# The second feed-forward's up projection as seven half-size products in eight of eleven steps, with its row factor in the operand and some arithmetic on GpSimd

## The reference

```python
h = rms_norm_2(x, norm_ffn_g[l])
up = causal_dwconv(h @ w_up[l], conv_ffn_w[l])      # w_up: 1024 x 5632, three taps along the tokens
a, b = jnp.split(up, 2, axis=-1)                    # 2816 channels each
x = x + (jax.nn.silu(a) * b) @ w_down[l]
```

## Time and profile before

| | |
|---|---|
| median of 3 runs | 1296.87 us (1295.75 to 1297.6) |
| the profiled execution's own time | 1296.4 us |
| its span in the profile | 1294.7 us |
| granted TensorE clock over the span | 0.999 of full speed |
| busy: PE, DVE, ACT, POOL | 98%, 69%, 45%, 10% |
| first up projection, PE | 240.2 to 461.0 us |
| second up projection, PE | 932.7 to 1175.7 us |

### The profile page before, as it was taken

One profiled execution on the slowest core, in us unless ns is written; L12 is line 12 of the kernel. 1 busy time (PEld: TensorE's weight loads), 2 busy tenths in 40 slices (PEclk: granted clock), 3 DMA queues, 4 the chain that ended last, 5 costly groups with the idle time before them and its releaser, 6 DMA issues.

```text
span 1294.7 us, 17058 instructions
## 1 busy us (share of the span) xinstructions
PE 1270.2 (98%) x6810; PEld 1064.7 (82%) x6810; DVE 893.9 (69%) x1062; ACT 588.5 (45%) x704; POOL 130.6 (10%) x120
## 2 busy tenths in 40 slices
PE   7999999999999999999999999999999999999997
PEld 5777677789999899998888888668888888888876
DVE  6788655887888688887536433658665656668796
ACT  6372672564554445564311322563433333336555
POOL 4003010013222010200000002000300000001020
PEclk9999999999999999999999999999999999999999
DMA  5422101259999497823433332102222222256765
GB/s 168 136 75 88 66 1 59 88 147 179 202 197 179 106 236 230 151 63 113 163 98 98 98 98 98 65 1 74 91 97 97 97 97 97 97 186 104 205 107 137
DMA packets 120708, 151.81 MB, mean 117 GB/s; under 512 B 4170, under 2 KB 93498, under 8 KB 120514
## 3 DMA queue, kind: packets, MB, share of 16 engines
q1 hardware_dynamic: 91906, 108.92, 25.2%
q0 software_dynamic: 28720, 41.96, 19.1%
q10 hardware_dynamic: 16, 0.00, 0.0%
HBM read 148.76 MB, written 2.11 MB: 117 GB/s over the span
## 4 chain that ended last, share of the span: by engine, by line
PE 95%; DVE 2%; ACT 2%; DMA 0%; issue 0%; SPq 0%; ACTq 0%
PE psum L1897 20%; PE psum L1899 20%; PE psum L1898 20%; PE psum L2158 4%; PE psum L2159 4%; PE psum L2160 4%; PE psum L2202 3%; PE psum L2354 3%; PE psum L2204 3%; PE psum L2356 3%; PE psum L2355 3%; PE psum L2203 3%; PE psum L2037 1%; PE psum L2022 1%; PE psum L2268 1%; PE psum L2049 1%
## 5 line engine op out<-in xcount | busy, mean ns | idle before, releaser
L1897 PE MATMUL psum<-act_hi,w_hi 128*128 128x512 f32 x968 | 385.1, 398 | 4.2 <-DVE act_lo L1191 1.7
L1898 PE MATMUL psum<-act_lo,w_hi 128*128 128x512 f32 x968 | 378.6, 391 | 0.0
L1899 PE MATMUL psum<-act_hi,w_lo 128*128 128x512 f32 x968 | 378.5, 391 | 0.0
L778 ACT ACTIVATE w_hi<-raw 128x2048 fp32r<-128x2048 f32 (+1 forms) x104 | 167.0, 1606 | 396.5 <-PE psum L1899 370.5
L1182 DVE TENSOR_TENSOR w_lo<-raw,w_hi 128x2048 fp32r<-128x2048 f32 (+1 forms) x104 | 199.4, 1918 | 63.2 <-ACT w_hi L778 63.2
L1897 PEld LDWEIGHTS psum<-act_hi,w_hi 128*128 128x128 f32 x968 | 181.8, 188 | 48.7 <-issue 6.5
L1899 PEld LDWEIGHTS psum<-act_hi,w_lo 128*128 128x128 f32 x968 | 181.8, 188 | 41.2
L1898 PEld LDWEIGHTS psum<-act_lo,w_hi 128*128 128x128 f32 x968 | 181.9, 188 | 39.5 <-issue 1.7
L2202 PE MATMUL psum<-part_hi,w_hi 128*128 128x256 f32 x308 | 86.3, 280 | 0.0
L2204 PE MATMUL psum<-part_hi,w_lo 128*128 128x256 f32 x308 | 85.9, 279 | 0.0
L2203 PE MATMUL psum<-part_lo,w_hi 128*128 128x256 f32 x308 | 85.9, 279 | 0.0
(11 more groups left out here) (334 smaller groups left out, 2270.2 us busy)
## 6 DMA issues: line engine op xcount, KB each, us to landing
raw<-in_w_in SPq DMA_DIRECT2D x30, 1024.0 KB, 5.1
raw<-in_w_up SPq DMA_DIRECT2D x22, 1024.0 KB, 5.0
xz<-in_w_ffn_in POOLq DMA_DIRECT2D x24, 512.0 KB, 6.5
raw<-in_w_ffn_in SPq DMA_DIRECT2D x22, 512.0 KB, 5.3
x_buf<-in_w_ffn_out POOLq DMA_DIRECT2D x6, 1024.0 KB, 9.2
x_buf<-in_w_down POOLq DMA_DIRECT2D x6, 1024.0 KB, 9.8
raw<-in_w_out SPq DMA_DIRECT2D x4, 1024.0 KB, 4.9
xz<-in_w_ffn_in SPq DMA_DIRECT2D x8, 512.0 KB, 5.4
```

The source lines that it names most:

```text
L778: A(w_at(w_hi, s, h, n - h), home(s, n)[:, h:n], ACT.Copy).then_inc(w_hi_ready, 1)
L1897: mm(dst, stationary[0], moving[0], start=first, stop=False)
L1898: mm(dst, stationary[0], moving[1], start=False, stop=False)
L1899: return mm(dst, stationary[1], moving[0], start=False, stop=last)
```

## The change

It gives the second up projection the same form as the first: steps 0, 1 and 10 stay as they were (step 10 in quarters), steps 2 to 9 become seven products each. Four things differ from the first up projection:

- the row factor is multiplied into the operand ahead of the products: ACT writes `xg`, the activations times the gain, for all eight chunks; POOL multiplies each by the row factor, makes the four sums in unused rows of `hid`, and ACT and DVE make `s_hi`, `s_lo` from these and overwrite `act_hi`, `act_lo` quarter by quarter;
- there is a convolution after the products: ACT makes the first tap (`gate_taps`, `up_taps`), DVE the two others (`gate_convolve`, `up_convolve`), both from SBUF;
- POOL makes one of the four blocks of each step (`gates[:, :, HALF:]`, signalled by `z_m1`) and the final products of the gate and up side (`hidden_rows`), two of 128 x 512, one step later;
- the loops are written out, and step i's gate side waits in ACT for `z_m1`; ACT copies p1 away only after `z_m1` of the step before, since `kept_1` is one buffer.

The core of the diff:

```diff
+def _second_up_order():
+    order = [("gate", 0), ("up", 0), ("gate", 1), ("up", 1), ("p0", 2), ("p1", 2), ("p2", 2), ("p4", 2)]
+    for i in range(FIRST_SEVEN + 1, LAST):
+        order += [("p0", i), ("p3", i - 1), ("p2", i), ("p5", i - 1), ("p1", i), ("p6", i - 1), ("p4", i)]
+    return order + [("gate0", LAST), ("gate1", LAST), ("p3", LAST - 1), ("p5", LAST - 1), ("up0", LAST), ("up1", LAST),
+                    ("p6", LAST - 1)]
...
 @block.gpsimd
+            for c in range(DC):
+                pool.wait_ge(xg_ready, DC + c + 1)
+                g.tensor_tensor(xg[:, c], xg[:, c], rstd[:, RSTD_AT[N_FFN2]], ALU.mult).then_inc(xg_scaled, 1)
+            second_sum(0, xg_block(0, 1), xg_block(1, 1))
...
+            for f in range(4, len(SECOND_UP_ORDER)):
+                kind, i = SECOND_UP_ORDER[f]
+                if kind == "p5":
+                    n = SEVENS + i - FIRST_SEVEN + 1
+                    pool.wait_ge(z_rest2, n)
+                    pool.wait_ge(z_k1, n)
+                    g.tensor_tensor(gates[:, :, HALF:], pair(rest_2), pair(kept_1), ALU.add).then_inc(z_m1, 1)
+                if f + 4 < len(SECOND_UP_ORDER) and SECOND_UP_ORDER[f + 4][0] in NEXT_OF:
+                    add_second(*SECOND_UP_ORDER[f + 4])
+                if kind == "p0" and i >= FIRST_SEVEN + 2 or kind == "gate0":
+                    hidden_rows(i - 2)
...
 @block.scalar
+            for c in range(DC):
+                A(xg[:, c], xT[:, c], ACT.Copy, scale=col("norm_ffn_g_2", c)).then_inc(xg_ready, 1)
+            splits(S_UP)
...
+            for e in range(S_UP + 5, S_DOWN2):
+                kind, i = SECOND_UP_ORDER[e - S_UP]
+                if kind in ("p0", "p1", "p2"):
+                    keep_second(kind, i)
...
+                splits(e)
...
+                if kind == "p1" and i > FIRST_SEVEN:
+                    gate_taps(i - 1)
+                if kind == "p6" and i < LAST - 1:
+                    up_taps(i)
+                if kind == "p4" and i > FIRST_SEVEN:
+                    gate_silu(i - 1)
...
 @block.vector
-            with dve.Fori(0, FFN_STEPS - 1) as i:
-                up_step(i, lambda: split_w(S_UP + 2, i), lambda: split_w(S_UP + 3, i))
...
+            for e in range(S_UP + 5, S_DOWN2):
+                kind, i = SECOND_UP_ORDER[e - S_UP]
+                finished(e)
+                if kind in BLOCK:
+                    recombine_second(kind, i)
...
+                splits(e)
...
+                if kind == "p1" and i > FIRST_SEVEN:
+                    gate_convolve(i - 1)
+                if kind == "p4" and i > FIRST_SEVEN:
+                    up_convolve(i - 1)
...
 @block.tensor
+                if kind == "p2":
+                    pe.wait_ge(z_k0, n)
...
+                if kind == "p4":
+                    pe.wait_ge(z_k1, n)
```

383 lines of the change are left out of this document (327 added, 56 removed).

## The result

The changed kernel takes **1319.39 us** (median, 1319.03 to 1322.51), the kernel before 1296.41 beside it: ratio 1.0182, 95% interval 1.0164 to 1.0199. It is 1.8% slower. The prediction was 1298.0 with a range of 1284 to 1307, so the time lies 12 us above the range and 21.4 us above the forecast.

The account below looks back on a forecast made before the run. PE was taken to bound the kernel, others counting only where PE waits. The stretch: 242.9 - 23.5 (fewer products) + 6.6 (start) + 18.0 (loop) = 244.0, 1.1 us more; total 1298.0 us, range 1284 to 1307.

Parts of the forecast that it names:

- the unit costs: Second up projection: distances between instruction starts on DVE, ACT and POOL, such as 1.14 us for DVE's half-size w_lo.
- the pattern of the loop: Steady steps: one dependency chain round all queues, with PE waiting 3.26 us a step, before p2 and p4.
- The loop's length: Steady steps: 22.3 us a loop against PE's 19.04; five loops and a last wait cost 18.0 us.
- Step (2): Loop, hidden_rows: DVE's w_lo delays POOL's first product to 4.85, DVE's next w_lo ends at 5.85, second product at 7.0.
- Step (3): Loop, POOL: DMA issue for p5 from 7.1 to 8.4, only then the z_m1 block, 8.5 to 9.8.
- PE gets to the p2 of step 4 without a wait: First seven-product steps: the pattern needs a step to build up, so no waiting is charged before p2 of step 4.
- The start: First up slab to p0 of step 2: waits of 1.6, 1 and 4, together 6.6 us, bounds 2 and 10.
- the holding up: Start: POOL's arithmetic delays DVE instructions; 1.3 us before p0, upper bound 10 with each sum against one instruction.
- A: Second up projection: PE bound as in the first, only the start costs; 1278 us, chance 0.10 together with D.
- B: Loop binds, but POOL and DVE don't meet, hidden_rows falls into gaps; loop 20.8, total 1289 us, chance 0.16.
- C: Loop: accumulating DMAs' landing comes into it, about 1 to 2 us longer each; + 8, total 1306 us, chance 0.17.
- D: Loop: 24 products each cost DVE 1.04, so DVE is at 19.0 a step; 1280 us, chance 0.10 with A.

Follow-up runs that it names:

- x1: Changed kernel with the block of gates (p5's rest plus kept p1) made on DVE instead of POOL; 1313.03 us, ratio 1.0108.
- x2: Changed kernel with POOL's two hidden products of every loop step replaced by fills with zeros; 1303.20 us, ratio 1.0047.
- x4: Changed kernel with a second buffer for the kept p1; 1307.34 us, ratio 1.0077.
- x3: Changed kernel with POOL's block of gates made ahead of the accumulating DMA issue that stood before it; 1320.08 us, ratio 1.0166.
- x8: Changed kernel with POOL's start multiplications cut to one column and its four sums replaced by fills; 1307.69 us, ratio 1.0082.
- x10b: x6 with the start's arithmetic on DVE, gate silu behind the kept p0, third down projection slab split ahead of the up taps; 1294.13 us, ratio 0.9972.
- x5: x1 with the loop's hidden rows also moved from POOL to DVE; 1305.75 us, ratio 1.0055.
- x6: x5 with x4's two buffers for the kept p1; 1304.27 us, ratio 1.0047.

## Right and wrong, by the prediction's steps

**What bounds it, the unit costs, the pattern of the loop: right.** PE waits before p2 and p4 of each step, for ACT's copies of p0 and p1, and ACT for POOL's block. x1, x2 and x4 take three different links out and each shortens the loop, x1 and x2 by what the link loses (1.65 and 2.77 us, 1.66 and 2.75 measured).

**The loop's length: right in kind, 0.7 us low (22.99 against 22.3).** Step (2) failed on who waits. POOL's next instruction starts 0.77 after a DMA issue begins (1082.76 to 1083.53), not after its 1.27. So the first product was under way when DVE began its w_lo, and DVE waited for both, 2.77 us, where the step let POOL wait first and DVE then about 1. The products ended at 5.35 (1083.53 + 3.07 - 1081.25), not at 7.0, and w_lo of p4 at 7.58 (1087.62 + 1.21), not at 5.85. The sum that the block needs stands behind that w_lo, ready at 8.2 and not 6.5. Step (3) then charged 1.3 for the DMA issue ahead of the block and 1.3 for the block. x3 shows that the issue costs nothing there; the block, held by a w_lo of DVE's, took 1.85. It was ready at 10.55 (1091.80), not at 9.8: that is the 0.7. Two terms were wrong in opposite directions and nearly made up for each other, so that the length came out so near is partly luck. In five loops and the last wait 19.9 us against 18.0.

**"PE gets to the p2 of step 4 without a wait": wrong, and the largest miss (11.8 us against 0).** The kept p1 lies in the row that the second step's taps still use, so ACT waits for up_hidden 4 before it copies p1 of step 2, and PE 3.83 us before p4. The diff shows that wait, and I passed over it since I followed only the chain of the steady loop. x4, which moves the row (and takes the wait for the block of the step before out of steps 3 to 7), has p4 of step 4 start 49.9 us after p0 of step 2 in place of 58.0. The first p4 of the loop waited too (1.34 us at 1046.56). Behind both long waits PE ran at 1.2 GHz: the first 27 matmuls behind the 5.58 us took 5.88 us, against 3.2 at 0.118 each, and the 24 of p4 of step 2 took 4.50, against 2.8. Of the 11.8 us the two waits are 5.2, the slow matmuls 4.4, and 1.8 are the 17 products at 0.118 us a matmul: the prediction's 19.04 for a step was itself too low here, the step's matmuls take 19.8.

**The start: right in place, 4.2 us low (10.8 against 6.6).** The third slab waited 0.35, not 1.6; the next 2.52, not 1; p0 of step 2 5.58, not 4. Of the remaining 2.3 us, 1.4 are the 1.2 GHz behind the wait of 2.52 (seven starts 0.43 us apart from 970.87 on, 0.23 otherwise); the rest I can't place. But PE's rate did not set the length: in x2 and x4 the clock stayed at full speed there, PE waited 7.3 us before p0 in place of 5.58, and the start took 55.91 and 55.94 all the same. DVE sets it. The failed term is the holding up, "1.3 for POOL" in the last piece and a bound of 10 with each sum against one instruction: a sum of 1024 elements on POOL takes 2.4 to 4.3 us and DVE's next instruction waits for what is left of it. DVE's records are longer by some 11.5 us in all than in x8: 4.1 in the first four taps, which take turns with POOL's multiplications, 0.2 and 2.1 in the third and fourth slab's w_lo, 2.1 and 3.0 in two taps behind them. x8 removes it and with it 10.5 us.

**The down projection: 3.1 us, charged nowhere**, though named at the prediction's end as a place to look. The third slab's w_hi stood behind the up taps in ACT's queue, and those behind DVE. x10b gets 2.9 us by the order of two lines.

**The rivals.** A (PE bound) fell: even without POOL's arithmetic in the loop the products take 156.7 us, where 144 (53 products at 2.72) was its price. B (no meeting) fell: 3.99 us for w_lo. C (the landing of the accumulating DMA) did not happen in the changed kernel; but when POOL's arithmetic is gone and the steps are shorter, it comes: ACT's w_hi waits for such DMAs in the loops of x5 and x6, 0.2 to 1.7 us a time, the DMA of p5 takes up to 10.0 us to land (x6, 1097.54), and the loop of x6 leads through that of p3. C named a link that binds only when the others are out. D gave DVE 19.0 us a step, and it is busy for 18.8 of 22.99 there; but that was no bound, since it is less than the loop, and 1280 did not follow.

**A slip in the sum.** 8 x 22.0 less 8 x 19.04 is 23.7, not 23.5, which changes nothing.

**The range** was taken from the bounds of the loop and the start; with both at their upper ends it was 1305. What lay outside was in stretches to which I gave no bound at all.

## What to carry to other kernels

Handing VectorE's arithmetic with two SBUF operands to an idle GpSimd can cost more than it relieves: here 10.5 us in the start and 2.75 us a step, and VectorE did the same work itself with PE waiting less (in the start with another order as well). When a new pipeline is put in, walk through its first step and its last one with the buffers they share with the old code, not only through the steady loop. And when a queue's order is changed to end a wait, find what is next in that queue before counting the gain: three orders of the start moved the wait from p2 to p4 and to p3, and none was cheaper than the first.
